# Another table of places for the attention half-steps of a two-layer transformer kernel

## The reference

```
h = rmsnorm(x, norm1_g);  p = h @ w_in                     # 1024 -> 2560
a = pool_mixer(p[:, :256])
b = diff_attention(p[:, 256:1792])     # 4 heads, two softmaxes each, causal
c = stick_breaking_attention(p[:, 1792:])   # 4 heads, exp(cumsum(log(1-beta))), causal
x = x + concat(a, b, c) @ w_out
x = x + (silu(h2 @ w_gate) * (h2 @ w_up)) @ w_down         # 1024 -> 2816 -> 1024
x = rmsnorm(x, final_norm_g)
h = rmsnorm(x, g_pre) * (1 + scale) + shift                # second layer
p = h @ w_in_2                                             # 1024 -> 3584
y = concat(gmlp_branch(p), retention_branch(p))            # chunks of 128 tokens
x = x + gate * rmsnorm(y @ w_out_2, g_post)
```

## Time and profile before

| | |
|---|---|
| runs | 3722.33, 3728.07, 3732.39 us |
| profiled execution | 3722.33 us, span 3720.7 us |
| TensorE (PE) busy | 3607.2 us, 97% |
| VectorE (DVE), ScalarE (ACT), GpSimd (POOL) busy | 1887.3, 1683.5, 802.0 us |
| chain that ended last | PE 87%, DVE 5%, ACT 3%, DMA 2% |
| granted clock, mean | 0.989 |
| TensorE idle, 3720.7 less 3607.2 | 113.5 us |

### The profile page before, as it was taken

The page is one execution under the profiler, slowest core; times in us unless marked ns, Lnnn a source line. Parts: engine busy times, 40 slices in busy tenths (PEclk is TensorE's granted clock), DMA queues, the critical chain, the costliest instruction groups (busy, mean ns, idle before and its releaser), DMA issues.

```text
span 3720.7 us, 51945 instructions
## 1 busy us (share of the span) xinstructions
PE 3607.2 (97%) x19752; PEld 3106.6 (83%) x19752; DVE 1887.3 (51%) x4056; ACT 1683.5 (45%) x3457; POOL 802.0 (22%) x704
## 2 busy tenths in 40 slices
PE   8999999999999999999999999999999999999998
PEld 7888888888887898888878888888878988888797
DVE  4346564554656665446655555434568752111443
ACT  4334654556655554445644444434456642111322
POOL 3444333554444331100011010110000000000100
PEclk9999999999999999999999999999999999999999
DMA  6877667677776667545454555555454464545454
GB/s 181 259 242 226 201 198 246 236 271 260 265 274 214 208 237 296 187 169 193 165 190 147 181 201 201 178 192 186 143 215 153 142 241 181 196 179 202 173 188 151
DMA packets 328203, 759.82 MB, mean 204 GB/s; under 512 B 53138, under 2 KB 212882, under 8 KB 271635
## 3 DMA queue, kind: packets, MB, share of 16 engines
q1 hardware_dynamic: 266898, 720.83, 55.7%
q10 hardware_dynamic: 61056, 35.67, 3.7%
HBM read 581.00 MB, written 175.39 MB: 203 GB/s over the span
## 4 chain that ended last, share of the span: by engine, by line
PE 87%; DVE 5%; ACT 3%; DMA 2%; ACTq 1%; issue 1%; POOL 0%; SPq 0%; DVEq 0%
PE PS L1442 24%; PE PS L1444 23%; PE PS L1443 23%; PE PS L1550 3%; PE PS L1560 3%; PE PS L1541 2%; PE PS L1542 2%; PE PS L1574 2%; PE PS L1520 1%; DVE BIG L2030 1%; ACTq L1781 1%; ACT BIG L1735 1%; DMA KVF<-in_w_ada 0%; ACTq L1766 0%; POOL WF L2429 0%
## 5 line engine op out<-in xcount | busy, mean ns | idle before, releaser
L1442 PE MATMUL PS<-BIG,WF 128*128 128x512 f32 (+1 forms) x1792 | 684.3, 382 | 7.9 <-DVE BIG L2030 6.5
L1444 PE MATMUL PS<-BIG,WF 128*128 128x512 f32 (+1 forms) x1792 | 673.2, 376 | 0.0
L1443 PE MATMUL PS<-BIG,WF 128*128 128x512 f32 (+1 forms) x1792 | 672.7, 375 | 0.0
L1442 PE MATMUL PS<-WF,BIG 128*128 128x256 f32 (+1 forms) x1888 | 646.6, 342 | 10.1 <-POOL WF L2429 5.1
L2429 POOL TENSOR_TENSOR WF<-RAW,WF 128x512 fp32r<-128x512 f32 x380 | 504.0, 1351 | 640.8 <-ACT WF L1680 640.5
L1444 PE MATMUL PS<-WF,BIG 128*128 128x256 f32 (+1 forms) x1888 | 632.2, 335 | 0.0
L1443 PE MATMUL PS<-WF,BIG 128*128 128x256 f32 (+1 forms) x1888 | 631.6, 335 | 0.0
L1442 PEld LDWEIGHTS PS<-WF,BIG 128*128 128x128 f32 x1888 | 361.0, 191 | 48.7 <-ACT BIG L1724 5.2
L1442 PEld LDWEIGHTS PS<-BIG,WF 128*128 128x128 f32 x1792 | 339.9, 190 | 68.3 <-ACT BIG L1735 4.8
L1444 PEld LDWEIGHTS PS<-BIG,WF 128*128 128x128 f32 x1792 | 339.3, 189 | 62.4
L1443 PEld LDWEIGHTS PS<-WF,BIG 128*128 128x128 f32 x1888 | 361.1, 191 | 36.2 <-issue 1.9
(11 more groups left out here) (230 smaller groups left out, 6250.6 us busy)
## 6 DMA issues: line engine op xcount, KB each, us to landing
WF<-scratch_WS SPq DMA_DIRECT2D x264, 1024.0 KB, 5.0
scratch_WS<-WF SPq DMA_DIRECT2D x110, 1024.0 KB, 6.7
W<-scratch_WS SPq DMA_DIRECT2D x66, 1024.0 KB, 5.0
RAW<-in_w_in SPq DMA_DIRECT2D x84, 512.0 KB, 4.7
KV<-scratch_KS SPq DMA_DIRECT2D x60, 512.0 KB, 5.8
QQ<-scratch_QS SPq DMA_DIRECT2D x192, 128.0 KB, 5.0
XH<-in_x SPq DMA_DIRECT2D x32, 512.0 KB, 7.1
scratch_QS<-STG ACTq DMA_DIRECT2D x96, 128.0 KB, 3.8
```

The costliest lines, as they stand in the source:

```text
L1442: pe.matmul(o, Ah, Bh, start=first, stop=False)
L1443: pe.matmul(o, Ah, Bl, start=False, stop=False)
L1444: return pe.matmul(o, Al, Bh, start=False, stop=last)
```

## The change

Only the digits of `HALF_STEPS` change. Both tables have 1452 digits that sum to 749, so the same half-steps run in the same order among themselves, and the matmuls of the projections run in the same order among themselves; only how the two are dealt together is new. The first 77 digits are all 0 in both tables. At most 16 half-steps are late in the new table against the old one at any place, and at most 14 early. One line of the fifteen:

```diff
 HALF_STEPS = (
-    "0000000000000000000000000000000000000000000000000000000000000000000000000000000001202021021011020200"
+    "0000000000000000000000000000000000000000000000000000000000000000000000000000010000111121120202000201"
 )
```

More of the change, by code:

```diff
@@ new lines @@
+    "0100422022200001030001614242110110200310031121040380020010000010020100011000001202021000010000000002"
+    "3121101100010000000020002013000020200101000001011001010000200020000002100010401102227000000000031000"
+    "0001200201101100100012212000102201002000000000001010001300200101001010021112111011100011000002000011"
+    "1000000100000000301042400001003010203110100000000100000000000010000000401010000020000011000001100020"
+    "4020100000000010001201010010010000000000100100020000100000101101000010000000100002002002000002000200"
@@ new lines @@
+    "0000000100001100101001010110200200110202001101101002122003020100118000102120120000001002000001010010"
+    "0000100100100100120120031110020002000000010200100200000100011120112111011100003000030110100010001012"
+    "0000200220111100112210101000000010000000110020000120100260111010021010000110000001010001000000000010"
+    "0000010001020000001000000200000000000010120200020000031001101001100010200001001010030103002011000010"
+    "0001000010000200000000020001000000000000010000010101013102003100300020011000210001000020010012100010"
@@ L231 @@
+    "0001123000100220000001010002001000011000031001000000100010000222222111130050000010001120000100000100"
+    "0200200201212200001000100200001110110010000200020010110000200000000001020000000100010100001100101210"
+    "1020310101000000000010010001000001001000000000200010011110010120120000200001101022231011100020010110"
+    "0000100020000200210010011002010110000100102110101317"
 )
```

## The result

The changed kernel takes 3770.85 us, the median of four runs (3767.28 to 3772.35), against 3730.23 us for the kernel before in the same comparison. The ratio is 1.0116, with a 95% interval of 1.0104 to 1.0129: 41 us slower. Over 23 executions of the changed kernel the median is 3772.26 us, and in the later comparisons that of the kernel before is some 3726.5, so the difference may be nearer 45 us. 3722.8 us was forecast, so neither the sign nor the range held.

A forecast was written before the change was run, and what follows sets the result against it. TensorE, busy 3607.2 of 3720.7 us, was taken as the bound, so only its gaps could move. The terms summed to -5.3 us against the median 3728.07, giving 3722.8 us; range 3711 to 3735, with outer rivals in part 3703 to 3742.

The forecast's parts named there:

- First score, gain 3.8 us: At the first score, earlier loads let the turning behind it go on 5.8 us sooner, less 2 us of low clock.
- "pre" tokens of chunk 0, gain 3.9 us: At chunk 0's "pre" tokens, waits of 7.35 us shrink to chunk 3's 3.48 us as fewer half-steps stand there.
- Turn of tile 155, gain 2.8 us: In chunk 1, TensorE's 2.81 us wait goes, since the combine now stands ahead of a late gMLP output on VectorE.
- Retention norm, gain 1.6: Behind a retention norm of chunk 0, a 1.42 us wait and 0.2 us of refilling go, the score standing later.
- Stacks, loss 4.8 us: Places with three or four scores in a row cost 6.4 us in the new table against 1.6 in the old.
- First `gmlp_mix`, loss 2.0 us: At chunk 0's first `gmlp_mix`, attention work now ahead of VectorE's norm lengthens TensorE's 2.54 us wait by 2.0 us.
- Turn of chunk 3's tokens, 0: At places 118 to 126, one wait around ScalarE's value stores is exchanged for another: 0, bounds -4 and +4 us.
- The faster rival: Whole kernel about 3713 us: stacks cost only 2 us and uncosted small waits worth some 7 us clear; chance 0.27.

The follow-up runs named there:

- first_77: Old table with only the first half-step (eleven attention loads, no score) moved from place 81 to 77, against the kernel before: 3734.28 us (1.0019).
- best_b: best_a plus new digits at places 99 to 126, the score of 495 at 497, and tile 155's combine moved ahead: 3704.48 us (0.9940).
- best_a: Old table with the first half-step at place 76 and the stick-breaking value stores issued by SyncE instead of ScalarE: 3709.77 us (0.9952).
- spread: New table with all sixteen places of three or four scores cut to two, the rest written at the next place: 3770.1 us (1.0123).
- tile15_early: New table with the half-step that turns tile 15 at place 118 instead of 121, and one more at 120 instead of 122: 3777.01 us (1.0141).
- Off_pool: New table with the three half-steps of place 137 at 139 and the one of 143 at 145: 3773.69 us (1.0126).
- first_73: Old table with only the first half-step (eleven attention loads) at place 73 instead of 81, against the kernel before: 3732.32 us (1.0016).
- first_76: Old table with only the first half-step (eleven attention loads) at place 76 instead of 81, against the kernel before: 3725.72 us (1.0005).

## Why the prediction was wrong, point by point

*What bounds the kernel.* Right: only TensorE's gaps moved. But the gaps that I priced were those that I could see in the old trace. A table that sets the order of 749 half-steps against 1452 pieces makes new ones, and the sum had a term for such only at stacks of scores and at the first `gmlp_mix`. That is the step that failed for the result as a whole: "Each term is one wait that goes, comes or changes its size" was applied to the waits of the old trace, and every wait without a row there was put at nothing, without a reason. The two traces put these at some 40 us.

*First score, gain 3.8 us: a loss of 3.7.* The step that failed is "ScalarE is then busy with its stores of values: 14 of them end at 291.91". The loads that I moved ahead were taken to change nothing for the others. They doubled the stores, 16.46 us for 8.10, which first_77 shows alone. The queries waited 2.80 us where I had about 1, and the transposes 9.31 where I had about 4. The Trainium skill's rule to issue early (DMA: Bandwidth & Descriptors, "Overlap DMA with compute") would have been further off still: first_77 follows it and is slower, since an early load isn't free for those who issue transfers beside it.

*"pre" tokens of chunk 0, gain 3.9 us: 0.2* (places 457 to 465 lose 10.3 us for 10.5). The step that failed is "7.35 less 3.48": chunk 3 was no measure for chunk 0. The 3.48 us of the earlier trace rows are only idle time; with the low clock behind it those three places lose 6.5 us, and the chain that comes last is 1.3 us longer in chunk 0, where weights are split beside it. And the wait of 1.56 us in the earlier trace rows is not the one of 5.71: it stands in front of line 1442, behind the first half's turning. The second half's transposes, which waited the 5.71 us in chunk 0, do not wait at all in chunk 3:

```profile
3488.35 0.60 PE L1520 MATMUL PS<-CB,XS 128*128 128x128 f32 x4
```

The wait of 1.56 us, and the half clock behind it (granted 0.50 from 3479.0 to 3484.3), had put off TensorE until the chain's end at 3488.23. So the two chunks' waits could not be set off one against the other. The attention in the earlier trace rows was beside the wait, not its main cause.

*Turn of tile 155, gain 2.8 us: right in its mechanism,* a little small in its size. Places 967 to 992 lose 1.5 us for 5.5, 4.0 where the upper bound was 3, and no wait of line 1550 for the combine is left. *Retention norm, gain 1.6: 0.9* (places 491 to 500, 1.4 for 2.3; the stack at 500 is in it). best_b takes such waits singly and is 5 us under best_a by the medians, though their intervals overlap. Its trace bears out two of its three pieces: places 99 to 126 lose 3.2 us less than in best_a and 967 to 992 lose 5.0 less. Places 491 to 500 lose the same 2.0 us (by line and shape), at 498 where it was at 495: the score moved from 495 to 497 took its wait along.

*Stacks, loss 4.8 us: 5.9,* and the bounds of 2 and 13 held. As a cause of the result they are out, by spread.

*First `gmlp_mix`, loss 2.0 us: 2.5, right* (places 523 to 530; the wait is 4.6 us for 2.54). *Turn of chunk 3's tokens, 0: +1.0* (places 118 to 126, 12.0 for 11.0), within its bounds; and the view of one wait for another was right there, as tile15_early shows from the other side.

*The sum.* By my terms' own places the outcome is +3.7 - 0.2 - 4.0 - 0.9 + 5.9 + 2.5 + 1.0, 8 us, where -5.3 was forecast. The two traces differ by 47.6 us. So my terms were 13 us off, and the other 40 us are waits that had no term (33 to 37 by the medians of the two kernels). Most are small: 124 places lose more than 0.3 us, where 93 did, from chunk 0's stick-breaking heads to the feed-forward part under chunk 3's attention. The faster rival named small waits that the new table would clear, for "near each place where TensorE must wait for a norm the new digits are 0 more often". That was read from the digits; the reverse happened.

*What is shown and what isn't.* Shown: the loss adds up over places, it isn't the stacks, and only the smaller part of it passes through stores and loads; a shift by one place of digits that are otherwise the old ones, and as dense, costs as much, in the two stretches where it was tried; and at the places opened above the mechanism is an instruction that stands in an engine's order behind one whose input is late. Not shown: that every one of the small waits is of this kind. In one of them (the turn of tile 19, line 1583, 3.32 us) instructions also took longer. VectorE's copies of line 2077 took 1.40 us each where they took 0.42 before. Off_pool did not settle why, but the two traces tell the cases apart; the kernel before, then the changed one:

```profile
495.92 0.42 DVE L2077 COPY XH<-XH 64x512 f32<-64x512 f32 x1
...
497.01 2.98 POOL L2429 TENSOR_TENSOR WF<-RAW,WF 128x512 fp32r<-128x512 f32 x2 [3.34 <-ACT WF L1680]
```

```profile
501.11 3.78 POOL L2429 TENSOR_TENSOR WF<-RAW,WF 128x512 fp32r<-128x512 f32 x2 [4.79 <-ACT WF L1680]
...
501.72 1.40 DVE L2077 COPY XH<-XH 64x512 f32<-64x512 f32 x1
```

Before, both copies (the second at 496.99) had already started when GpSimd's split of weights began at 497.01; in the changed kernel both started while one ran. Line 2084, a few instructions later, has it the other way round: it started inside a split and took 1.40 us before, and ahead of one and took 0.49 us after. So what a piece meets sets not only the order but also the length of instructions. How much of the 40 us comes by this way was not measured.

## What to carry to other kernels

In a kernel whose order is written by a table, a change of the table is judged by what each moved instruction stands behind on its own engine afterwards, not by how many stand together; a shift by one place is a cheap measure of what a rearrangement can cost (18 and 22 us here). A wait that the profile blames on a transfer or an engine can cover the next one a few us later, as at the first score and at the turn of tile 15, so look for who else uses the moved resource in that window, and change the partners together: the loads at 76 and the stores on SyncE gave 0 and 5 us alone and 17 us together.

## What the runs showed of the hardware

Issuing a store can hold ScalarE for long, and the price is not always the same. The 14 stores of 64 KB took 7.25 us at a DMA share of 0.59, 8.10 at 0.89 and 16.46 at 1.08. These are the windows over first_73's stores, over those of the kernel before, and, shown above, over the changed kernel's:

```profile
291.33:298.58 7.25, 5.92 (x51) 5.71 (x49) 2.51 (x8) 0.25 (x1) 0.00 (x0) 1.00 0.59 126
```

```profile
283.81:291.91 8.10, 1.76 (x15) 1.55 (x13) 1.28 (x3) 0.26 (x1) 0.00 (x0) 0.85 0.89 209
```

first_76 had 1.10 over its own 9.35 us, though, so a full set of DMA engines isn't enough: there the eleven loads had all been issued before the first store, at 283.05 the last of them six microseconds ago, while in the changed kernel and first_77 the two queues issued side by side at first. The trace of the changed kernel shows that issuing side by side isn't needed either. Its last eight stores, and SyncE's last issue of the burst with the one that follows it:

```profile
289.05 10.06 ACTq L1781 DMA_DIRECT2D scratch_VS<-STG  x8
```

```profile
288.32 1.17 SPq L2638 DMA_DIRECT2D scratch_GWS<-GB  x1
299.30 0.33 SPq L2634 DMA_DIRECT2D GB<-in_gmlp_ws  x1
```

These eight stores took 10.06 us, 1.26 each, and from 289.49 on SyncE issued nothing beside them. What is left is that the loads had been issued shortly before: at a median of 8.5 us from issue to landing for the keys and 8.4 for the values, the last of them were under way for some of these ten us. That was not tried by itself.
